# Attention of one transformer kernel: alternating two differential heads and making the scores of two steps from four row groups

## What is computed

```python
def one(args):                                    # diff_attention, for a block of 128 queries
    qi, pi = args
    sc = jnp.einsum('bhcqe,bhcke->bhcqk', qi, k).astype(jnp.float32) * scale
    dist = jnp.abs(pi[:, :, None] - pos[:, None, :]).astype(jnp.float32)
    sc = sc - slopes[None, :, None, None, None] * dist[:, None, None]
    a = jax.nn.softmax(sc, axis=-1)
    return jnp.einsum('bhqk,bhkv->bhqv', a[:, :, 0] - lam * a[:, :, 1], vf)
```

## Time and profile before

| what | value |
|---|---|
| median of three runs | 3258.81 us |
| the profiled execution, its own time | 3258.92 us |
| its span | 3257.2 us |
| TensorE busy | 3211.0 us, 99% |
| VectorE busy | 1849.5 us, 57% |
| ScalarE busy | 514.0 us, 16% |
| mean granted TensorE clock | 0.994 of full |
| attention, layer 0 | 1515.4 to 1655.8 us of the span |
| attention, layer 1 | 2652 to 2793 us of the span |

### The profile page before, as it was taken

The page is one execution under the profiler, slowest core; times in us unless marked ns, Lnnn a source line. Parts: engine busy times, 40 slices in busy tenths (PEclk is TensorE's granted clock), DMA queues, the critical chain, the costliest instruction groups (busy, mean ns, idle before and its releaser), DMA issues.

```text
span 3257.2 us, 35901 instructions
## 1 busy us (share of the span) xinstructions
PE 3211.0 (99%) x14194; PEld 2556.8 (78%) x14194; DVE 1849.5 (57%) x3204; ACT 514.0 (16%) x1068; POOL 226.4 (7%) x197
## 2 busy tenths in 40 slices
PE   9999999999999999999899999999999998999999
PEld 3888744888888888884478888888888744788888
DVE  6357835664337764453766664466644537766643
ACT  2111121000001000114521000110001145210001
POOL 1244400000000000003000000000000030000000
PEclk9999999999999999999999999999999999999999
DMA  5244311222222222223012222222222230122221
GB/s 235 91 172 164 117 52 45 72 91 91 88 84 91 82 86 84 97 73 123 1 52 79 90 91 81 88 91 91 84 88 88 73 123 1 53 91 79 90 81 62
DMA packets 43207, 286.16 MB, mean 88 GB/s; under 512 B 5248, under 2 KB 5248, under 8 KB 12064
## 3 DMA queue, kind: packets, MB, share of 16 engines
q1 hardware_dynamic: 39024, 271.14, 23.5%
q0 software_dynamic: 4016, 12.73, 1.2%
HBM read 279.66 MB, written 2.10 MB: 87 GB/s over the span
## 4 chain that ended last, share of the span: by engine, by line
PE 92%; DVE 5%; DVEq 1%; ACT 1%; issue 1%; DMA 0%; ACTq 0%; POOL 0%
PE ps L847 76%; PE ps L555 4%; PE ps L536 3%; PE ps L1226 2%; PE ps L1194 1%; PE ps L874 1%; DVE arena L1820 1%; PE ps L954 1%; DVE arena L2213 1%; ACT arena L1521 1%; PE ps L1208 1%; DVEq L2226 1%; PE ps L1233 0%; PE ps L1165 0%; PE ps L1158 0%
## 5 line engine op out<-in xcount | busy, mean ns | idle before, releaser
L847 PE MATMUL ps<-arena 128*128 128x256 f32 x5456 | 1245.1, 379 | 0.7 <-DVE arena L1911 0.6
L847 PEld LDWEIGHTS ps<-arena 128*128 128x128 f32 x5456 | 1036.3, 190 | 142.8 <-DVE arena L1911 1.6
L847 PE MATMUL ps<-arena,ring 128*128 128x256 f32 x2768 | 646.3, 379 | 0.5 <-ACT arena L1266 0.5
L847 PEld LDWEIGHTS ps<-arena,ring 128*128 128x128 f32 x2768 | 525.6, 190 | 72.5 <-ACT arena L1266 0.9
L847 PE MATMUL ps<-xn,ring 128*128 128x256 f32 x2272 | 520.7, 380 | 5.8 <-DVE arena L1636 2.4
L847 PEld LDWEIGHTS ps<-xn,ring 128*128 128x128 f32 x2272 | 432.3, 190 | 72.4 <-issue 9.6
L1630 DVE TENSOR_TENSOR arena<-arena,ps 128x512 f32<-128x512 f32 x169 | 116.0, 687 | 537.2 <-PE ps L847 508.1
L1606 DVE TENSOR_TENSOR arena<-ring 128x512 f32<-128x512 f32 (+1 forms) x190 | 128.3, 675 | 347.5 <-PE ps L847 347.2
L847 PE MATMUL ps<-xn,arena 128*128 128x256 f32 x1264 | 302.2, 379 | 0.0
L847 PEld LDWEIGHTS ps<-xn,arena 128*128 128x128 f32 x1264 | 240.2, 190 | 32.7
L1433 ACT ACTIVATE arena<-arena 128x512 f32<-128x512 f32 x88 | 55.5, 630 | 883.6 <-DVE arena L2091 883.5
(11 more groups left out here) (312 smaller groups left out, 2359.0 us busy)
## 6 DMA issues: line engine op xcount, KB each, us to landing
ring<-in_w_up_a SPq DMA_DIRECT2D x44, 1024.0 KB, 4.8
ring<-in_w_up_b SPq DMA_DIRECT2D x44, 1024.0 KB, 4.8
ring<-in_w_ff SPq DMA_DIRECT2D x32, 1024.0 KB, 4.8
ring<-in_w_ada SPq DMA_DIRECT2D x24, 1024.0 KB, 4.9
ring<-in_w_down_a SPq DMA_DIRECT2D x16, 1024.0 KB, 4.9
ring<-in_w_down_b SPq DMA_DIRECT2D x16, 1024.0 KB, 4.8
ring<-in_w_in SPq DMA_DIRECT2D x14, 1024.0 KB, 4.9
ring<-in_w_out SPq DMA_DIRECT2D x12, 1024.0 KB, 4.9
```

The lines of the kernel that those rows point to most:

```text
L847: mm = nc.tensor.matmul(out_ap, w, operand(product, quads[i]), start=at not in opened, stop=last_chunk and i == len(quads) - 1, skip_group ...
```

## The change

The four query blocks of two C heads of a pair now alternate: head 0 block 0, head 1 block 0, head 0 block 1, and so on. In an even C step TensorE issues four score matmuls, from the four row groups into all four score banks, for this step and the next, with one increment of `scores` after each two; in the odd step it issues none. It waits for the minima of step n - 1 in place of n - 2, since all four banks must be free. VectorE gets a further wait before `least` of an odd C step: the transposes of step n - 4 must have read the probability buffers, which the order of the PE queue no longer ensures. Which engine copies a turned unit stays a matter of the step's parity. The first B step after a C block waits as before for the step two back.

```diff
 def step(n):
     kind, g = ATT_GROUPS[n // ST]
+    if kind == "C":
+        at = n - ST * (n // ST - g % 2)
+        return kind, g - g % 2 + at % 2, at // 2
     return kind, g, n % ST
+
+def c_map(n):
+    return step(n)[1] % 2
...
-                    if n > 1:
-                        name = "exps" if step(n - 2)[0] == "B" else "minima"
-                        pe.wait_ge(sem(name), UNITS_2 * layer + 2 * (n - 2) + 2)
+                    if kind == "C" and c_map(n):
+                        return
+                    before = n - 1 if kind == "C" else n - 2
+                    if before >= 0:
+                        name = "exps" if step(before)[0] == "B" else "minima"
+                        pe.wait_ge(sem(name), UNITS_2 * layer + 2 * before + 2)
...
-                    for u in range(2):
+                    for u in range(4 if kind == "C" else 2):
...
-                            r = slice(64 * (g % 2) + 32 * u, 64 * (g % 2) + 32 * u + 32)
+                            r = slice(32 * u, 32 * u + 32)
...
-                        mm = nc.tensor.matmul(ps[:, 2 * (n % 2) + u, :], q, k, start=True, stop=True)
-                    mm.then_inc(sem("scores"), 1)
+                        mm = nc.tensor.matmul(ps[:, (2 * (n % 2) + u) % BANKS, :], q, k, start=True, stop=True)
+                        if u % 2:
+                            mm.then_inc(sem("scores"), 1)
...
                     dve.wait_ge(sem("scores"), ATT_STEPS * layer + n + 1)
...
+                    if kind == "C" and c_map(n):
+                        u = c_map(n - 4) if step(n - 4)[0] == "C" else 1
+                        wait_turned(dve, (layer, "turn", n - 4, u))
```

More of the change, by code:

```diff
@@ L262, in turn_uses @@
                 kind, _, i = step(n - 3)
-                for u in ((i % 2,) if kind == "C" else (0, 1)):
+                for u in ((c_map(n - 3),) if kind == "C" else (0, 1)):
                     use((layer, "turn", n - 3, u), ("act", "dve")[u])
@@ L1193, in scores @@
                             q, k = q_b[:, 2 * g + u, qs], k_b[:, 2 * g + u, :]
-                        mm = nc.tensor.matmul(ps[:, 2 * (n % 2) + u, :], q, k, start=True, stop=True)
-                    mm.then_inc(sem("scores"), 1)
+                        mm = nc.tensor.matmul(ps[:, (2 * (n % 2) + u) % BANKS, :], q, k, start=True, stop=True)
+                        if u % 2:
+                            mm.then_inc(sem("scores"), 1)
                 def turn(n):
                     kind, _, i = step(n)
-                    for u in ((i % 2,) if kind == "C" else (0, 1)):
+                    for u in ((c_map(n),) if kind == "C" else (0, 1)):
                         unit = 2 * n if kind == "C" else 2 * n + u
@@ L1526, in turned @@
                     kind, g, i = step(n)
-                    if kind == "C" and i % 2:
+                    if kind == "C" and c_map(n):
                         return
@@ L2237, in turned @@
                     kind, g, i = step(n)
-                    if kind == "C" and i % 2 == 0:
+                    if kind == "C" and not c_map(n):
                         return
```

## The result

| kernel | median of 20 runs | lowest to highest |
|---|---|---|
| before | 3258.14 us | 3251.83 to 3259.75 |
| changed | 3263.45 us | 3257.92 to 3267.85 |

The medians differ by 5.3 us where the forecast had 5.1. The ratio, estimated from the same runs, is 1.0019, with a 95% interval of 1.0013 to 1.0025, that is 6.2 us, 4.2 to 8.1, on the edge of what was called "no change". Something is lost, though little. Medians in this document are over all runs, ratios leave out the single far slower executions (4825.76 us in `after_warm_scores`, for one).

A forecast was written before the change was run, and what follows sets the result against it. VectorE was taken to bound the C blocks, except at the A1 weighing. Wait 0.5, half clock at scores 3.2 and at weighings 1.4 made 5.1 us on 3258.92: 3264.0 us, called "same", range 3258 to 3271.

The forecast's parts named there:

- What bounds it: C blocks: the chain runs on VectorE, except at the A1 weighing on TensorE; cheaper scores lie beside VectorE's work.
- (a): C scores: four groups cost 1.06 us a pair of steps; TensorE loses 17.0 us of work, worth 0.
- (b): C scores wait for the step just before instead of two back: 0.12 us a block, 0.5 us in all.
- the clock at the scores: Longer TensorE rest puts the scores VectorE awaits at half clock: 0.8 us a block, 3.2 us in all.
- (c): VectorE's added wait for the transposes of step n - 4: 2.4 us in hand at full clock, so 0.
- (d): The changed order of heads: counts of joins, copies, transposes and banks by parity stay, so 0.
- The weighing: A1 weighing behind a 2.2 us rest may meet half clock: 1.4 us, 4 in 10 for each layer's first block.
- Rival 1: C blocks: the clock's fall reaches the weighing, 1.71 us each; 3267.3 us in two blocks, 3270.7 in four; chance 0.36.
- Rival 2: C blocks: clock falls no earlier than now, or delayed scores escape it; only 0.5 us stay, 3259.4 us; chance 0.14.
- rival 3: C scores: the four groups run two after two, half the clock's cost goes; 2.8 us longer, 3261.7 us; chance 0.08.
- rival 4: Attention: TensorE is the bound after all, its 17.0 us come off; 3241.9 us; chance 0.04.

The follow-up runs named there:

- after_warm_scores: The changed kernel with 4 spare matmuls before the last four-group scores of each C block; 3258.40 us, 1.0008 of the kernel before.
- lead_one: The kernel before with only the wait changed: C scores wait for the minima of step n - 1, still two units a step; 3270.70 us, ratio 1.0039.
- after_warm_both: The changed kernel with spare matmuls in TensorE's rests, 2 before the A1 weighing and 4 before each C block's last scores; 3257.86 us, ratio 1.0006.
- order_only: The kernel before with only the alternating order of the two heads, two units of scores a step and the old wait; 3254.77 us, ratio 0.9993.
- before_late2_act2: before_late2 with two more copies of turned units of each C block on ScalarE in place of VectorE; 3252.72 us, 0.9991 of the kernel before.
- after_late2_act2: after_late2 with two more copies of turned units of each C block on ScalarE in place of VectorE; 3246.89 us, 0.9971 of the kernel before.
- before_late2: The kernel before with weighings one step later except a layer's last two pairs, and head sums two steps behind ScalarE's squares; 3252.83 us, ratio 0.9982.
- after_late2: The changed kernel with weighings one step later except a layer's last two pairs, and head sums two steps behind ScalarE's squares; 3251.36 us, ratio 0.9982.

## Why the prediction was right, step by step

- **What bounds it.** Held. TensorE lost 12.1 us of busy time in the attentions, the 17.0 forecast for the scores less what the rows at half clock added, and none of it reached the end. (The 19.1 us of the whole span hold 7.0 that the change doesn't touch.)
- **(a), four groups at 1.06 us a pair.** Measured 1.07 to the next instruction. The 1.19 us estimated from the Trainium skill, "TensorE: Matmul & The Clock Gate", section on packing small matmuls, was too high here. "Worth 0" is right for the sum as made. `lead_one` shows that it is 0 only as the rest of a larger loss: alone, the shorter lead costs 13.8 us in the attentions, nearly all of it at half clock, the groups give 6.5 back. The prediction priced lead and groups together by way of the pair, so the sum didn't suffer.
- **(b) and the clock at the scores.** Forecast 0.12 + 0.8 us a block, 3.7 in all; measured 1.07, 1.10, 1.07, 0.73, that is 3.97. The rests foretold at 3.9 and 4.6 us were 3.99 and 4.65. I took 0.8 between bounds of 0 and 1.13; three blocks paid some 0.95. The 0.12 alone is confirmed by `after_warm_both` (2.53 against 2.41 us).
- **(c), the wait for transposes.** 0, held: no wait at `least` of odd steps.
- **(d), the order.** 0, held by `order_only`: attentions 140.35 and 140.98.
- **The weighing.** The rest was 2.32 us, 2.2 foretold. Size off in the profile: 1.4 us forecast (4 in 10 of 1.71, for two blocks), 3.28 measured, both first blocks having paid in full. `after_warm_scores` shows blocks with the same rest that don't pay. The place was right: the second block of each layer was spared in the profile. The reason given for it, the work that lies between, wasn't what spared it in layer 0: there the clock fell at 1594 us, on the scores of 1.67 us and what followed, and was back at 1598, before the weighing at 1599.16.
- **Not foreseen:** the VectorE pause of 0.43 us (below), and 0.3 us won back at the end of layer 1.

By the profile the sum would be 7.3 where 5.1 was forecast; the medians say 5.3 and the ratio 6.2, 4.2 to 8.1. So in total the forecast is right within what can be told, and the scores' share is confirmed by the traces. That 5.1 and 5.3 agree so closely is luck: the share of the weighing was a chance of 4 in 10 written as 1.4 us, and the one profile had it in full. Rival 1 (both weighings pay, 8.4 us) is what the profiled execution did, less 1.1 us. Rival 2 (no earlier fall) and rival 3 (two after two) are refuted by the rows above, rival 4 by the time. That bursts between rests start at the half clock, as the section on HAM oscillation of the same page of the Trainium skill has it, held behind the four rests of 3.99 and 4.65 us, not behind that of 2.32 us in `after_warm_scores`. The rests in that section's example are waits of about 3 to 5 us, so the prediction read too much into it when it let all four weighings pay by it: the rest before them is 2.32 us in the first blocks.

## What to carry to other kernels

Work taken from an engine that waits for another anyway becomes rest, and on TensorE rest can cost the clock: price what the next run on the path takes at half clock, not only the wait. Before work is made in larger pieces, ask what lead it leaves; one step of lead instead of two, with the half clock that met it, cost more here than the packing saved. Look for the longest wait that remains and move work past that: shifting the weighing by a step, with the tail left alone, was worth what the packing was not.

## What the runs showed of the hardware

- Four row groups of 32 rows and 512 columns in f32 take the time of two: 1.07 against 1.06 us, two units each way.
- The clock can fall behind short rests: before the fall in the changed kernel's weighing TensorE had rested 2.32 us, and at 2692 us in `after_warm_scores` the rests before it were 1.45 and 0.34 us with transposes between, and so at 1594 us in the changed kernel (1.45 and 0.35 us). The same rest at the same place of the program led to a fall in one execution and to none in another.
- With plain full-array matmuls as filling, four or eight instructions at a time, the clock stayed at 1.00 through the whole block, rests of 0.34 to 1.45 us included; it didn't take a TensorE that never rests.
- VectorE pauses 0.43 us once a layer in the changed kernel, in front of a tiny operation of `join` (L2242) and with no releaser in the trace; the kernel before has 0.35 us, in layer 1 alone, in front of the 128x512 operation of `join` (L2230). The pause stands in `after_warm_both` too. Its cause stays open.
- Also open: why, with ScalarE's copies, `before_late2_act2` and `after_late2_act2` seem to part, where `before_late2` and `after_late2` don't.
